# Seven products for one more slab in two FFNs, and for five slabs in a third

## The reference, cut to what matters

```python
def swiglu(h, w1, w3, w2):                      # first model, blocks 0 and 1
    return (jax.nn.silu(h @ w1) * (h @ w3)) @ w2
x = x + mod_l[5] * swiglu(modulate(rmsnorm(x, ffn_norm_g[i]), mod_l[3], mod_l[4]), ffn_w1[i], ffn_w3[i], ffn_w2[i])
return rmsnorm(x, final_g)                      # end of the first model

def swiglu_2(h, w_in, w_out):                   # second model, two in each layer
    gate, up = jnp.split(h @ w_in, 2, axis=-1)
    return (jax.nn.silu(gate) * up) @ w_out
x = x + 0.5 * swiglu_2(rms_norm(x, ffn1_norm[l]), ffn1_w_in[l], ffn1_w_out[l])
x = x + 0.5 * swiglu_2(rms_norm(x, ffn2_norm[l]), ffn2_w_in[l], ffn2_w_out[l])
```

## Time and profile before

| | |
|---|---|
| median of 3 runs | 1638.15 us |
| the profiled execution | 1637.92 us, of which span 1636.6 us |
| TensorE busy | 1614.7 us (99% of the span), 7848 matmuls |
| VectorE busy | 1237.8 us (76%), 1480 instructions |
| ScalarE busy | 864.3 us (53%) |
| GpSimd busy | 343.6 us (21%) |
| DMA | 380.81 MB, mean 233 GB/s |
| granted TensorE clock | 1.0 of full speed |

### The profile page before, as it was taken

The page is one execution under the profiler, slowest core; times in us unless marked ns, Lnnn a source line. Parts: engine busy times, 40 slices in busy tenths (PEclk is TensorE's granted clock), DMA queues, the critical chain, the costliest instruction groups (busy, mean ns, idle before and its releaser), DMA issues.

```text
span 1636.6 us, 21299 instructions
## 1 busy us (share of the span) xinstructions
PE 1614.7 (99%) x7848; PEld 1304.6 (80%) x7848; DVE 1237.8 (76%) x1480; ACT 864.3 (53%) x1078; POOL 343.6 (21%) x501
## 2 busy tenths in 40 slices
PE   7999999999999999999999999999999999999999
PEld 3776788888778888788888888888888888888887
DVE  3898778897786764766888776679767988866687
ACT  3436654435475443544657554455544657564454
POOL 0002200001201231134403212441054304202350
PEclk9999999999999999999999999999999999999999
DMA  9788698898958876586675858758675784957763
GB/s 352 243 295 258 164 317 277 310 352 295 306 143 274 267 255 194 171 240 189 239 244 190 239 122 246 212 166 304 218 221 180 248 255 161 238 151 232 215 198 130
DMA packets 264118, 380.81 MB, mean 233 GB/s; under 512 B 17696, under 2 KB 198660, under 8 KB 264016
## 3 DMA queue, kind: packets, MB, share of 16 engines
q1 hardware_dynamic: 239744, 332.44, 61.6%
q0 software_dynamic: 21840, 42.51, 11.7%
q10 hardware_dynamic: 2432, 4.51, 0.8%
HBM read 363.92 MB, written 26.21 MB: 238 GB/s over the span
## 4 chain that ended last, share of the span: by engine, by line
PE 89%; DVE 5%; ACT 3%; issue 1%; DMA 1%; SPq 0%; DVEq 0%; ACTq 0%
PE bank L537 22%; PE bank L539 21%; PE bank L538 21%; PE bank L947 4%; PE bank L952 4%; PE bank L948 4%; DMA raw<-in_ada_w 1%; DVE lo L2113 1%; PE bank L1461 1%; PE bank L1462 1%; PE bank L1464 1%; PE bank L892 1%; PE bank L1269 1%; ACT hi L1517 1%; DVE XN L2577 1%
## 5 line engine op out<-in xcount | busy, mean ns | idle before, releaser
L2113 DVE TENSOR_TENSOR lo<-raw,hi 128x2048 fp32r<-128x2048 f32 x246 | 563.9, 2302 | 187.2 <-ACT hi L1517 186.0
L1517 ACT ACTIVATE hi<-raw 128x2048 fp32r<-128x2048 f32 x258 | 490.6, 1912 | 243.1 <-PE bank L539 146.9
L537 PE MATMUL bank<-hi,XTh 128*128 128x512 f32 (+1 forms) x1424 | 558.8, 392 | 1.7 <-DVE XTl L2248 1.3
L539 PE MATMUL bank<-hi,XTl 128*128 128x512 f32 (+1 forms) x1424 | 551.3, 387 | 0.0
L538 PE MATMUL bank<-lo,XTh 128*128 128x512 f32 (+1 forms) x1424 | 550.9, 387 | 0.0
L537 PEld LDWEIGHTS bank<-hi,XTh 128*128 128x128 f32 x1424 | 267.4, 188 | 66.0 <-issue 12.5
L539 PEld LDWEIGHTS bank<-hi,XTl 128*128 128x128 f32 x1424 | 267.4, 188 | 55.2
L538 PEld LDWEIGHTS bank<-lo,XTh 128*128 128x128 f32 x1424 | 267.5, 188 | 53.6 <-issue 1.0
L3200 POOL DMA_DIRECT2D HTR<-BLK x320 | 192.5, 610 | 490.3 <-DVE BLK L2673 416.3
L947 PE MATMUL bank<-hi,HTh 128*128 128x512 f32 x336 | 131.7, 392 | 0.0
L948 PE MATMUL bank<-lo,HTh 128*128 128x512 f32 x336 | 130.8, 389 | 0.0
(11 more groups left out here) (412 smaller groups left out, 2015.4 us busy)
## 6 DMA issues: line engine op xcount, KB each, us to landing
raw<-in_ffn_w_in SPq DMA_DIRECT2D x176, 512.0 KB, 4.9
raw<-in_ffn_w SPq DMA_DIRECT2D x132, 512.0 KB, 5.1
raw<-in_ada_w SPq DMA_DIRECT2D x96, 512.0 KB, 5.7
raw<-in_ffn_w_out SPq DMA_DIRECT2D x76, 512.0 KB, 4.2
raw<-in_w_mix_in SPq DMA_DIRECT2D x52, 512.0 KB, 4.9
sums<-in_ffn_w_out POOLq DMA_DIRECT2D x24, 512.0 KB, 8.9
raw<-in_od_pw_w SPq DMA_DIRECT2D x24, 512.0 KB, 7.5
raw<-sums SPq DMA_DIRECT2D x24, 512.0 KB, 4.8
```

What stands on the lines that cost most here:

```text
L537: pe.matmul(dst, xh, wh, start=start, stop=False)
L539: return pe.matmul(dst, xl, wh, start=False, stop=stop)
L1517: act.activation(hi[r][:, :], raw[g % RAW][:, :], ACT.Copy).then_inc(*up("hi", d))
L2113: dve.tensor_tensor(lo[r][:, :], raw[g % RAW][:, :], hi[r][:, :].bitcast(F32), ALU.subtract).then_inc(*up("lo", d))
```

## The change

It changes which slabs are fast, by FFN, in place of one rule for all:

- FFNs 6 and 8 get a seventh fast slab: 0, 1, 2, 4, 5, 6, 7 instead of 0, 1, 3, 4, 6, 7. Stored sums: 0, 2, 4, 5, 7 (before 0, 3, 6). Made: 1 and 6 (before 1, 4, 7). GpSimd makes the five stored sums in two groups, of three and of two, one behind the other.
- FFN 2 gets five fast slabs: 0, 1, 3, 5, 7, all with made sums. It had none. The shared sums there are multiplied by the gate before they are added to X (`shared_added`).
- FFNs 3 and 5 stay as they are.

```diff
-FAST = (3, 5, 6, 8)
-FASTS = (0, 1, 3, 4, 6, 7)
-STORED = (0, 3, 6)
-FAST_SPLIT_UP = {5: (2,), 6: (0, 1), 8: (5,), 9: (3, 4)}
-FAST_SPLIT_DOWN = {1: (8,), 3: (6, 7), 4: (9, 10)}
+FAST = {p: (0, 1, 3, 4, 6, 7) for p in (3, 5, 6, 8)}
+STORED = {p: (0, 3, 6) for p in FAST}
+SPLITS = {p: ({5: (2,), 6: (0, 1), 8: (5,), 9: (3, 4)}, {1: (8,), 3: (6, 7), 4: (9, 10)}) for p in FAST}
+LAST_COLUMNS = {p: 3 for p in FAST}
+FAST[2], STORED[2], LAST_COLUMNS[2] = (0, 1, 3, 5, 7), (), 2
+SPLITS[2] = {5: (2,), 6: (0, 1), 8: (4,), 9: (3, 5)}, {1: (6, 8), 2: (7,), 4: (9, 10)}
+for _p in (6, 8):
+    FAST[_p], STORED[_p] = (0, 1, 2, 4, 5, 6, 7), (0, 2, 4, 5, 7)
+    SPLITS[_p] = {6: (0, 1), 7: (2,), 8: (3,), 9: (4, 5)}, {1: (8,), 3: (6, 7), 4: (9, 10)}
...
-    down("down3", A["ffn_w2"][1, :, :])
+    down("down3", A["ffn_w2"][1, :, :], 2)
...
+            def shared_added(f, t):
+                sums = TR[:, t * D:(t + 1) * D]
+                if f == FFNS[2]:
+                    dve.wait_ge(*at("gate_full", (*FFN_GATE[2], 1)))
+                    dve.tensor_tensor(sums, sums, GATE[:, 1, :], ALU.mult).then_inc(*up("e_gated", (f, t)))
+                    dve.wait_ge(*at("e_gated", (f, t)))
+                    dve.tensor_tensor(X[:, t, :], X[:, t, :], sums, ALU.add).then_inc(*up("e_added", (f, t)))
...
+                for group in stored_groups(p):
...
+                    pool.wait_ge(*at("sums_made", (p, group[-1])))
```

More of the change, by code:

```diff
@@ L477, in col @@
             return COLS[:, vec[name]:vec[name] + n]
-        A["sums"] = {p: nc.dram_tensor(f"sums{p}", (len(STORED), P, SLAB), F32, kind="Internal").ap() for p in FAST}
+        A["sums"] = {p: nc.dram_tensor(f"sums{p}", (len(STORED[p]), P, SLAB), F32, kind="Internal").ap()
+                     for p in FAST if STORED[p]}
         slabs, first, dense, fast_at, stored_at, made_at = weight_slabs(A)
@@ L492, in down_at, with fast_batch, sums_slot, sums_own @@
         def down_at(p, s):
-            return first[f"down{p}"] + s + (sum(x < s for x in FASTS) if p - 1 in FAST else 0)
+            return first[f"down{p}"] + s + sum(x < s for x in FAST.get(p - 1, ()))
         def down_order(p):
-            kinds = [(s, (0, 1) if p - 1 in FAST and s in FASTS else (0,)) for s in range(DOWNS[p][0])]
+            kinds = [(s, (0, 1) if s in FAST.get(p - 1, ()) else (0,)) for s in range(DOWNS[p][0])]
             return [(down_at(p, s) + n, s, n) for s, parts in kinds for n in parts]
[L501 to L513, removed]
+        def fast_batch(p, i):
+            return next(n for n in range(3) if i in BATCH[p][n])
+        def sums_slot(p, i):
+            n = fast_batch(p, i)
+            return (i if len(FAST[p]) > 6 else (4, 6, 0)[n] + BATCH[p][n].index(i))
+        def sums_own(p, n):
+            i = BATCH[p][n][0]
+            return slice(sums_slot(p, i), sums_slot(p, i) + len(BATCH[p][n]))
+        def stored_groups(p):
+            return [STORED[p][n:n + 3] for n in range(0, len(STORED[p]), 3)]
         def sums_of(p):
@@ L894, in turn, with seven @@
                     last.then_inc(*up("turned", (p, t, h)))
-            def seven(f, d, s, i):
-                kk, batch = 2 * s, fast_batch(i)
-                begin, end = i == 0, i == len(FASTS) - 1
+            def seven(p, d, s, i):
+                f, kk, batch = FFNS[p], 2 * s, fast_batch(p, i)
+                begin, end = i == 0, i == len(FAST[p]) - 1
                 r, q = ready(d), (d + 1) % RING
@@ L932, in down @@
                 order = order or range(nslab)
+                normal = next(s for s in order if s not in FAST.get(p - 1, ())) if p else 0
                 def products(s, t, parts=(0, 1)):
@@ L945, in products @@
                         for m in parts:
-                            begin = n == 0 and s == (2 if p - 1 in FAST and t + m == 2 else 0)
+                            begin = n == 0 and s == (normal if t + m == 2 else 0)
                             pe.matmul(acc[t][m][:, :], sh, w[m][0], start=begin, stop=False)
@@ L2716, in ffn @@
                             ada_quarter(*unit)
-                if during is not None and p not in FAST:
+                if during is not None and p != 3:
                     during()
@@ L3269, in sync_engine @@
                 if split in stored_at:
-                    sp.wait_ge(*at("sums_made", (stored_at[split], STORED[-1])))
+                    p, s = stored_at[split]
+                    sp.wait_ge(*at("sums_made", (p, next(group[-1] for group in stored_groups(p) if s in group))))
                 for n, (dst, src) in enumerate(parts(raw[r])):
```

117 lines of the change are left out of this document (61 added, 56 removed).

## The result

| | before | after |
|---|---|---|
| median | 1638.16 us (7 runs, 1638.14 to 1638.39) | 1643.39 us (7 runs, 1643.22 to 1643.61) |
| profiled execution, span | 1637.92, 1636.6 | 1643.23, 1641.9 |
| TensorE, matmuls | 1614.7 us, 7848 | 1611.1 us, 7827 |
| VectorE busy | 1237.8 us | 1268.8 us |

The changed kernel is slower: ratio 1.0032, 95% interval [1.0022, 1.0041], or 5.2 us. The forecast was 1642.5 us with a range of 1638.8 to 1644.6.

What follows compares the result with a forecast made beforehand. TensorE bounds the kernel (busy 99% of the span), so the question was whether VectorE delivers. FFN 2 at -0.1 and FFNs 6 and 8 at +4.5 gave +4.4 us, from 1638.15 to 1642.5 us, 8-in-10 range 1638.8 to 1644.6.

Steps and rivals of the forecast that it cites:

- FFNs 6 and 8, first wait: In down7 and down9, VectorE needs 10.92 us to 6a against TensorE's 9.52, so TensorE waits 1.40 us.
- allowance: In down7 and down9, 0.15 us added for each wait, as an operation's end is seen later than start distances say.
- Second wait: In down7 and down9, TensorE is ready for 6b at 12.96, VectorE's split at 14.32: a wait of 1.36 us.
- The sum of the two stages: Each of down7 and down9 loses 2.76 us and saves 0.68; with 0.15 per wait, together +4.5 us.
- FFN 2: In down3 and the turn to up3, all of the 3.40 us saved turns into waits behind VectorE: -0.1 us.
- T: End of TensorE's last b entry, slab 7; in down3 predicted at 644.9 instead of 648.3.
- GpSimd and DMAs: The second stored-sums group takes 35 to 50 us within GpSimd's gap; 4 MB more DMAs per place: 0, up to +1.
- The shared port: FFN 2's added column sums on GpSimd beside VectorE: taken as 0; under an exclusive lock up to 1 us more.
- The waits don't occur: Rival: FFNs 6 and 8's waits are absent or small, 1636.7 us, with half of them 1639.4; chance 0.13.
- the saving goes through: Rival: VectorE is a full ring ahead at both places, all 4.76 us are saved, 1633.4 us; chance 0.05.
- FFN 2 keeps some of its gain: Rival: VectorE reaches down3's shared sums at T + 1.5, -1.5 us, with the waits 1641.1; chance 0.12.
- VectorE is slower than in my rows: Rival: down3's entries 5b and 7b are missed, or DMAs or port cost it, +1 to +3, 1644.5; chance 0.10.

Runs made afterwards that it cites:

- experiment 3: Changed kernel, in FFNs 6 and 8 the last column sums and columns 6, 7 one slab earlier, columns 9, 10 two slabs later: 1637.37 us.
- experiment 5: Changed kernel, but in FFNs 6 and 8 the made sums belong to slabs 1 and 4 (stored: 0, 2, 5, 6, 7): 1638.24 us.
- experiment 4: Changed kernel, but in FFNs 6 and 8 only the columns of slabs 9 and 10 made two calls later (call 6 instead of 4): 1642.11 us.
- experiment 1: Changed kernel without the new slabs of FFNs 6 and 8, so only FFN 2's part: 1638.25 us, ratio 1.0001 to the kernel before.
- experiment 8: Kernel before, with GpSimd also making two more slabs' stored sums in FFNs 6 and 8, which nothing reads: 1638.16 us.
- experiment 6: Changed kernel, with VectorE splitting up3's first slab while ScalarE squares X, instead of behind the scaling of X: 1642.72 us.
- experiment 7: Changed kernel with up3's split moved as in experiment 6, and FFN 2's first-block shared sums joined with the result before the gate multiplication: 1642.46 us.
- run 9: Changed kernel with the spread columns of experiment 3 and the shorter FFN 2 turn of experiment 7 together: 1636.11 us, ratio 0.9987 to the kernel before.
- experiment 2: Changed kernel without FFN 2's part, so only FFNs 6 and 8 have a seventh fast slab: 1643.21 us.
- run 10: Run 9 plus a seventh fast slab in FFN 5, with the spread columns: 1635.43 us, ratio 0.9983 to the kernel before.
- run 11: Seven fast slabs with spread columns in FFNs 5, 6 and 8, FFN 2 unchanged from the kernel before: 1636.35 us, ratio 0.9989.

## Why the prediction was right, step by step

**FFNs 6 and 8, first wait: right in mechanism, 0.3 us short in size.** TensorE begins slab 4 in `down7` at 1291.27. From VectorE's split of 5b (1293.57) to the end of 6a's (1302.44) the rows add up to 8.87 us, which is exactly the prediction's 10.92 less 2.05. What was mis-sized is the front: VectorE starts 2.30 us after slab 3, not 2.05, since ScalarE itself begins 0.25 late, in the row below. 6a starts at 11.40 against the predicted 11.07 with its allowance; less TensorE's 9.52 that is a wait of 1.88 against 1.55 (the profile lists 1.73, as it counts from the modelled end of the last matmul). Experiments 3 and 5 show the cause by taking either of its parts away.

```profile
1291.52 1.92 ACT L1530 ACTIVATE hi<-raw 128x2048 fp32r<-128x2048 f32 x1 [3.59 <-PE bank L965]
```

**Second wait: right.** 6b starts 3.41 us after 6a, with 2.04 of matmuls between: 1.37 against 1.36. Experiment 4 shows it by itself.

**The sum of the two stages** was put at +4.5 us. In the traces `down7` loses 2.38 and `down9` 2.69, and a wait in the mixer stage between them (0.27 us, of which 0.23 remain) adds the rest: 5.3.

```profile
1434.69 0.88 PE L1373 MATMUL bank<-FT,UM 128*64 128x128 f32 x12 [0.27 <-DVE FT L2958]
```

The prediction has nothing for the mixer stage. Per stage the allowance of 0.15 for latencies was too small; 0.3 to 0.6 would have been right. That term (0.6 us) and the 0.23 make the difference between 1642.5 and 1643.39.

**FFN 2: right.** T 645.35 (predicted 644.9); VectorE at the shared sums 647.94 (647.8); shared sums 7.43 us (7.35); result's rows 655.37 (655.1); X ready 660.9 (660.7); gain 663.06 (662.9). Experiment 1 gives +0.1 us for this part where -0.1 was taken. Of the two places where the 3.40 us were to come back, the first has a wait of 1.89 us as listed, 2.05 by the starts (as the prediction counts), where some 2.3 was forecast. X came 0.2 us later than counted, but TensorE reached T 0.45 late (645.35 against 644.9), 0.19 of which it had before FFN 2 began. The rest is at `up3`'s first products and behind them: TensorE's listed waits from 658 to 680 us add up to 3.53 us (1.89, 0.44, 0.63, 0.57) against 0.91 before (0.30, 0.61).

**GpSimd and DMAs: right, 0.** The first and the last operations of the added group in `up8`, and the next move:

```profile
1447.27 0.54 POOL L3164 DMA_DIRECT2D sums<-in_ffn_w_out  x1 [6.26 <-DMA sums<-sums]
...
1481.49 1.65 POOL L3178 DMA_DIRECT2D sums<-sums  x2 [7.94 <-DMA sums<-sums]
1496.42 2.51 POOL L3227 DMA_DIRECT2D HTR<-BLK  x4 [13.28 <-DVE BLK L2697]
```

With the landing of the last additions (6.3 and 9.1 us from their issue) the group takes about 44 us, in the predicted 35 to 50. So of the 13.28 us ahead of the next move some 8 are this landing, and about 5 us of the gap are left. Experiment 8 confirms the 0.

**The shared port.** The added column sums do slow VectorE: three of its rows just ahead of `down3`, beside GpSimd's four operations from 600.78 to 604.5:

```profile
601.07 0.84 DVE L2108 TENSOR_TENSOR raw<-raw,raw 128x512 f32<-128x512 f32 x1
601.84 0.94 DVE L2123 TENSOR_TENSOR lo<-raw,hi 128x512 fp32r<-128x512 f32 x1
602.70 1.48 DVE L2124 TENSOR_TENSOR lo<-raw,hi 128x1024 fp32r<-128x1024 f32 x1
605.59 0.75 DVE L2730 TENSOR_TENSOR HID<-SG,bank 128x256 f32<-128x256 f32 x2 [1.41 <-ACT SG L1852]
```

```profile
601.32 0.91 POOL L3207 TENSOR_TENSOR SR<-HTR 128x128 f32<-128x128 f32 x1
602.19 0.91 POOL L3209 TENSOR_TENSOR SR<-SR,HTR 128x128 f32<-128x128 f32 x1
```

Without company these three take 0.69, 0.68 and 1.22, so 0.67 us is lost, and it vanishes in the time that VectorE idles next (1.41 us are left). The prediction's sentence by the Trainium skill (SBUF — State Buffer, "Who interferes with whom"), an exclusive lock worth up to 3 us here, allowed +1 us. The measurement decides: VectorE's rows are longer by 0.15 to 0.26 us beside operations of 0.58 to 1.33 us, not by a whole operation, and the time lost nothing. It was so in the earlier trace rows too, where VectorE lost 0.43 us beside an operation of 1.18, so "the trace agrees" holds for the slowing and not for its size.

**Rivals.** "The waits don't occur" and "the saving goes through" fell with the two pairs of waits. "FFN 2 keeps some of its gain" fell with experiment 1. "VectorE is slower than in my rows" would have lost in `down3`; no TensorE wait stands there.

**Left open.** Why the wait in the mixer stage comes and goes. It stands, with 0.27 to 0.29 us, in the profiles of the changed kernel, of experiments 3 to 7 and of run 9, and in none of the others: the kernel before, experiments 1, 2 and 8, runs 10 and 11.

## What to carry to other kernels

Where two engines meet through a ring, count the fuller engine's work between the moment the ring frees a slot and the moment the other needs the entry; its busy share over the stage says nothing. Work that speeds the bound engine shortens that time, so spread the helpers' small tasks before adding it: here the same operations in another order were worth 6 us, and three more fast slabs 1.8. And a chain that is full on the helper (VectorE in `down3`) turns every matmul saved into waiting until the chain itself is shortened.

## What the runs showed of the hardware

**The granted clock after a wait of about 2 us.** TensorE's wait ahead of the transposes was followed by a granted clock of 0.50 in the profiles of experiments 1, 6, 7 and run 10, and by 1.00 throughout in those of the changed kernel and of 3, 4, 5 and run 9. In this order the waits were 1.90, 2.49, 2.11 and 2.11 us with the fall, and 1.89, 2.50, 1.96, 1.90 and 2.11 without. So over 1.9 to 2.5 us the length of the wait does not say whether the clock falls; with 0.30 us (the kernel before) it did not. The profile of run 9, at the same place with the same wait as run 10, is the contrast to experiment 6:

```profile
661.08 1.09 PE L904 MATMUL bank<-IDENT,X 128*128 128x128 f32 x8 [2.11 <-DVE X L2634]
```

```profile
662.00:663.00 1.00, 1.00 (x7) 0.82 (x6) 1.00 (x2) 0.50 (x1) 0.00 (x0) 1.00 0.92 259
```

A fall costs the transposes 0.3 to 0.9 us, which shows in the time only where TensorE, not VectorE, is then the later one. With the shorter turn it is: from the transposes before FFN 2 to those behind the turn, run 9's profile gains 1.30 us on the kernel before, run 10's, with the same turn and the fall, 0.61. With the long turn it isn't: the changed kernel (no fall) and experiment 1 (fall) both gain 0.16.

**A transfer's delay that put VectorE back by 0.57 us showed at the shared sums 37 us later undiminished** (experiment 3): on the way there VectorE has a single gap, of 0.35 us, in both executions.
